# Three of four groups of each ungated MLP: the second product as seven half-size products, interleaved with the next group's first product

## The reference, cut to what matters

```python
def sqrelu_mlp(h, w_up, w_down):
    u = jnp.einsum('bsd,df->bsf', h, w_up)
    return jnp.einsum('bsf,fd->bsd', jnp.square(jax.nn.relu(u)), w_down)
...
x = x + sqrelu_mlp(rmsnorm(x, norm_mlp[l]), w_up[l], w_down[l])
```

## Time and profile before

| what | value |
|---|---|
| median of 3 runs | 1828.68 us (1828.45 to 1829.08) |
| the profiled execution | 1827.43 us |
| its span, first to last instruction | 1825.6 us |
| mean granted TensorE clock | 0.994 |
| PE busy | 1777.6 us, 97% |
| DVE busy | 959.8 us, 53% |
| ACT busy | 749.0 us, 41% |
| POOL busy | 104.7 us, 6% |

### The profile page before, as it was taken

One profiled execution on the slowest core, in us unless ns is written; L12 is line 12 of the kernel. 1 busy time (PEld: TensorE's weight loads), 2 busy tenths in 40 slices (PEclk: granted clock), 3 DMA queues, 4 the chain that ended last, 5 costly groups with the idle time before them and its releaser, 6 DMA issues.

```text
span 1825.6 us, 21577 instructions
## 1 busy us (share of the span) xinstructions
PE 1777.6 (97%) x8447; PEld 1460.1 (80%) x8447; DVE 959.8 (53%) x1740; ACT 749.0 (41%) x1475; POOL 104.7 (6%) x151
## 2 busy tenths in 40 slices
PE   8999999999999999989999999999999999999998
PEld 7887888888887777767888888878787788888886
DVE  6656443434344667765434434379986544244345
ACT  7433342323233666754233323243767533223223
POOL 0000010101010021011010101000000000000000
PEclk9999999999999999999999999999999999999999
DMA  7222223333323212112333332323100333333331
GB/s 246 78 80 81 81 95 102 103 94 94 97 98 86 70 49 68 47 47 81 94 97 99 93 104 93 104 71 103 51 19 1 95 106 98 93 96 101 96 101 58
DMA packets 195748, 158.30 MB, mean 87 GB/s; under 512 B 5248, under 2 KB 161280, under 8 KB 195648
## 3 DMA queue, kind: packets, MB, share of 16 engines
q1 hardware_dynamic: 194240, 154.16, 27.4%
q0 software_dynamic: 400, 1.25, 0.3%
q10 hardware_dynamic: 1008, 1.53, 0.2%
HBM read 154.81 MB, written 2.10 MB: 86 GB/s over the span
## 4 chain that ended last, share of the span: by engine, by line
PE 89%; DVE 6%; ACT 3%; issue 1%; DMA 0%; POOL 0%; DVEq 0%; SPq 0%; ACTq 0%
PE ps L736 29%; PE ps L738 28%; PE ps L737 28%; PE ps L1171 1%; PE ps L792 1%; ACT sb L1635 1%; PE ps L1065 0%; DVE sb L1855 0%; DVE sb L1853 0%; ACT sb L1375 0%; DVE sb L1881 0%; PE ps L851 0%; DVE sb L2265 0%; DVE sb L2218 0%; PE ps L1036 0%
## 5 line engine op out<-in xcount | busy, mean ns | idle before, releaser
L736 PE MATMUL ps<-sb,sb 128*128 128x512 f32 (+3 forms) x2547 | 976.0, 389 | 9.2 <-ACT sb L1635 5.2
L738 PE MATMUL ps<-sb,sb 128*128 128x512 f32 (+3 forms) x2547 | 956.8, 380 | 0.0
L737 PE MATMUL ps<-sb,sb 128*128 128x512 f32 (+3 forms) x2547 | 956.3, 380 | 0.0
L736 PEld LDWEIGHTS ps<-sb,sb 128*128 128x128 f32 (+1 forms) x2547 | 472.8, 188 | 116.0 <-issue 13.6
L738 PEld LDWEIGHTS ps<-sb,sb 128*128 128x128 f32 (+1 forms) x2547 | 472.3, 188 | 91.2
L737 PEld LDWEIGHTS ps<-sb,sb 128*128 128x128 f32 (+1 forms) x2547 | 472.9, 188 | 85.9 <-issue 0.2
L1855 DVE TENSOR_TENSOR sb<-sb,sb 128x512 fp32r<-128x512 f32 x532 | 348.7, 695 | 342.7 <-ACT sb L1375 341.6
L1375 ACT ACTIVATE sb<-sb 128x512 fp32r<-128x512 f32 x532 | 305.9, 622 | 432.1 <-PE ps L738 430.7
L2073 DVE TENSOR_TENSOR sb<-sb,sb 128x512 fp32r<-128x512 f32 x64 | 68.1, 1064 | 176.9 <-ACT sb L1524 176.6
L1534 ACT ACTIVATE sb<-ps 128x512 f32<-128x512 f32 x64 | 38.3, 598 | 208.6 <-PE ps L738 208.6
L664 POOL TENSOR_TENSOR sb<-sb 128x512 f32<-128x512 f32 x64 | 66.8, 1043 | 786.5 <-ACT sb L1534 786.5
(11 more groups left out here) (210 smaller groups left out, 982.5 us busy)
## 6 DMA issues: line engine op xcount, KB each, us to landing
sb<-in_w_up SPq DMA_DIRECT2D x86, 512.0 KB, 3.9
sb<-in_w_down SPq DMA_DIRECT2D x86, 512.0 KB, 3.9
sb<-in_w_gate SPq DMA_DIRECT2D x22, 512.0 KB, 3.7
sb<-in_a_w_in SPq DMA_DIRECT2D x20, 512.0 KB, 3.7
sb<-in_w_in SPq DMA_DIRECT2D x20, 512.0 KB, 3.6
sb<-in_w_o SPq DMA_DIRECT2D x16, 512.0 KB, 3.9
sb<-in_w_mem_kv SPq DMA_DIRECT2D x8, 512.0 KB, 7.5
sb<-in_w_out SPq DMA_DIRECT2D x8, 512.0 KB, 3.9
```

The costliest lines, as they stand in the source:

```text
L736: mm(ps, lh, rh, start=start, stop=False, **k)
L737: mm(ps, lh, rl, start=False, stop=False, **k)
L738: return mm(ps, ll, rh, start=False, stop=stop, **k)
```

## The change

Groups 0, 1 and 2 of each MLP compute the second product as seven products of half size in each dimension (256 tokens by 512 features by 512 columns) of sums of quarters, in a form of Strassen's scheme; group 3 keeps the old second product. Product j of group g (`P`) and tile j of group g+1's first product (`U`) take turns on PE, with two tiles behind product 6.

- A product is two slabs of 12 matmuls each. The weight quarters are loaded by SP as eight DMAs of 256 KB a group into buffers `DB` of their own. DVE forms eight half-quarter sums of weights (`T`, 128x1024) and four sums of quarters of the activation (`S`, 128x1024).
- DVE evicts each `U` tile with relu and the norm factor in one instruction (`r`), ACT squares into `HF` (`q`), and the high and low parts of the seven left operands are written by ACT and DVE over 1024 columns at a time (`h`). DVE reads each product's two banks (`rd`).
- POOL no longer works in the MLPs. PE transposes the norm factor into bank 7 and ACT copies it to `RB` in each MLP (`spread`), behind tile 1 of group 0. ACT squares the last two token tiles of `X` ahead of turns 4 to 7.
- `weights` is written to convert the slabs of a set `WIDE` in one instruction (`parts = 2`), and all others in two.

The diff, cut to what matters:

```diff
+    PRODUCTS = [(4, 2, "11", 0), (6, 5, "21", 0), (4, 0, "T2", 2), (6, 1, "11", 1), (2, 6, "12", 3), (6, 3, "22", 0),
+                (2, 4, "21", 4)]
...
+        for m in range(8):
+            up_tile(l, 0, m)
+        for g in range(3):
+            for j in range(7):
+                PS[l, g, j] = len(slabs)
+                for a in range(2):
+                    QSLAB[len(slabs)] = (l, g, j, a)
+                    slabs.append(([], 2, 512, None, 0))
+                for m in [j] if j < 6 else [6, 7]:
+                    up_tile(l, g + 1, m)
...
+    WIDE = {i for i in QSLAB} | {i for k, i in SL.items() if k[0] == "up" and k[2] > 2}
...
+        for g in range(3):
+            n = g + 1
+            last = g == 2
+            plan += [("P", g, 0), ("U", n, 0), up(n, 0), ("r", g, 7), ("q", g, 7), ws(g, 1, 0), ("S", g, 1), ("h", g, 1),
+                     ws(g, 1, 1), ("rd", g, 0), ("S", g, 2)]
+            plan += [("P", g, 1), ("U", n, 1), up(n, 1), ("r", n, 0), ("h", g, 2), ws(g, 2, 0), ("h", g, 3), ws(g, 2, 1),
+                     ("rd", g, 1), ("S", g, 4)]
+            plan += [("P", g, 2), ("U", n, 2), up(n, 2), ("q", n, 0), ("r", n, 1), ("q", n, 1), ("h", g, 4), ws(g, 3, 0),
+                     ("T", g, 3, 0), ws(g, 3, 1), ("rd", g, 2), ("T", g, 3, 1)]
+            plan += [("P", g, 3), ("U", n, 3), up(n, 3), ("r", n, 2), ("q", n, 2), ("h", g, 5), ws(g, 4, 0), ws(g, 4, 1),
+                     ("rd", g, 3), ("T", g, 4, 0), ("T", g, 4, 1)]
+            plan += [("P", g, 4), ("U", n, 4), up(n, 4), ("r", n, 3), ("q", n, 3), ("h", g, 6), ws(g, 5, 0), ws(g, 5, 1),
+                     ("rd", g, 4)]
+            if last:
+                plan += [("hc", 0), ("hc", 1), ("fold", 0, 1)]
...
+            plan += [("P", g, 6), ("U", n, 6), ("U", n, 7), up(n, 6), ("r", n, 5), ("q", n, 5), up(n, 7)]
...
+                plan += [ws(n, 0, 0), ("rd", g, 6), ("r", n, 6), ("q", n, 6), ("T", n, 1, 0), ws(n, 0, 1), ("T", n, 1, 1),
+                         ("T", n, 2, 0), ("T", n, 2, 1)]
...
+        def load_quarter(l, g, b):
...
+            for a in range(2):
+                if g > 0:
+                    q.wait_ge(S("w_lo"), 2 * (PS[l, g - 1, j] + a) + 2)
...
+                e.dma_start(DB[b][a][:, :].rearrange("p (k c) -> p k c", k=2), src).then_inc(S(f"db{b}_{a}"), 16)
...
-            for m in range(32):
-                z = m % 2
-                q.wait_ge(S("relu"), 32 * l + m + 1)
-                q.wait_ge(S("h_lo"), 32 * l + m - 1)
-                TTT(T2[:, z, :], T1[:, z, :], T1[:, z, :], ALU.mult).then_inc(S("relu2"), 1)
...
+            def product(g, j):
+                b, out, _, _ = PRODUCTS[j]
+                ah, al = AR[(7 * g + j) % 4]
+                q.wait_ge(S("h_lo"), h_done(l, g, j))
+                for a in range(2):
+                    _, wh, wl = next_slab()
+                    for t in range(2):
...
+                        for r in range(2):
+                            k, x, w = 2 * a + r, slice(128 * t, 128 * t + 128), slice(512 * r, 512 * r + 512)
+                            m = mm3(banks[b + t][:, :], ah[:, k, x], al[:, k, x], wh[:, w], wl[:, w],
+                                    k == 0 and j in (0, 1, 3, 4), k == 3, skip=True)
+                    m.then_inc(S("w_used"), 1)
...
-            for x in range(at["lo"], 2 * min(to, NSLAB) + half):
-                i, h = x // 2, x % 2
+            while at["lo"] < 2 * min(to, NSLAB) + half:
+                i, h = at["lo"] // 2, at["lo"] % 2
+                parts = 2 if i in WIDE else 1
...
+                elif kind == "r":
...
+                    stt(T1[:, m % 2, :], banks[u_bank(g, m)][:, :], 0.0, RB[:, :], ALU.max, ALU.mult).then_inc(S("relu"), 1)
```

More of the change, by code:

```diff
@@ L382, in build @@
+    PLAN_M = [mlp_plan(l) for l in range(2)]
     CV_GROUPS = [range(0, 10), range(10, 20), range(20, 31)]
@@ L921, in mlp, with free @@
             turn_first(X, job)
-            def free(m):
-                if m < 4:
+            def free(g, m):
+                if g == 0 and m < 4:
                     q.wait_ge(S("res"), base - 4 + m + 1)
-                elif m % 8 < 4:
-                    q.wait_ge(S("res"), base + 8 * (m // 8) - 4 + m % 8 + 1)
-                else:
[L930 to L944, removed]
@@ new lines, in mlp, with bank_free @@
+            for step in PLAN_M[l]:
+                if step[0] == "U":
+                    g, m = step[1:]
+                    tile_t(Ah, Al, job, u_bank(g, m), lambda: free(g, m),
+                           turn_in_tile(X, job) if (g, m) == (0, 0) else no_step)
+                elif step[0] == "spread":
+                    q.wait_ge(S("turn_lo"), 8 * JOB[job] + 8)
+                    spread(X, job)
+                elif step[0] == "P":
+                    product(*step[1:])
+            for n in range(2):
+                order = [2, 3, 4, 5, 6, 7, 0, 1]
+                def bank_free(t):
+                    if n == 1 and t < 2:
+                        q.wait_ge(S("relu"), 32 * l + 31 + t)
+                    else:
+                        q.wait_ge(*out_done(l, 2, 6 if n == 1 else 2 if t < 2 else 5, t % 2))
+                tile_n(CH["down", l, n], Bh, Bl, lambda k: q.wait_ge(S("h_lo"), h_done(l, 3, order.index(k))),
+                       (4, 0)[n], bank_free, behind=behind if n == 1 else no_step)
@@ L1513, in mlp @@
                 turn(job, Ah, job, k)
+            for t in range(2, 4):
+                square(X, job, t)
             weights(SL["up", l, 0] + 2)
@@ L1516, in mlp @@
                 turn(job, Ah, job, k)
[L1517 to L1540, removed]
+            rsqrt(job, 4)
@@ new lines, in mlp @@
+            for step in PLAN_M[l]:
+                if step[0] == "w":
+                    weights(step[1])
+                elif step[0] == "spread":
+                    spread(1 + l)
+                elif step[0] == "q":
+                    g, m = step[1:]
+                    q.wait_ge(S("relu"), 32 * l + 8 * g + m + 1)
+                    if g > 0:
+                        q.wait_ge(S("h_lo"), h_done(l, g - 1, 3 if m < 4 else 6))
+                        q.wait_ge(S("hs"), 4 * (3 * l + g - 1) + 4)
+                    act(HF[:, m, :], T1[:, m % 2, :], ACT.Square).then_inc(S("h_sq"), 1)
+                elif step[0] == "h":
+                    g, j = step[1:]
+                    q.wait_ge(*a_ready(l, g, j))
+                    q.wait_ge(*a_free(l, g, j))
+                    act(AR[(7 * g + j) % 4][0], A_OF[j][0], ACT.Copy).then_inc(S("h_hi"), 1)
+                elif step[0] == "hc":
+                    m = step[1]
+                    q.wait_ge(S("h_sq"), 8 * (4 * l + 3) + m + 1)
+                    q.wait_ge(S("w_used"), PS[l, 2, 3 + m // 2] + 2)
+                    act(Bh[:, (m + 2) % 8, :], HF[:, m, :], ACT.Copy).then_inc(S("h_hi"), 1)
@@ L1542, in scalar_program @@
+            for n in range(2):
+                for j in range(4):
+                    weights(CH["down", l, n].first + j + 3)
         mlp(0)
@@ L1807, in scalar_program @@
                 if m == 0:
-                    spread(2)
+                    spread(4)
                 if m > F0[g]:
@@ L2069, in mlp @@
                 turn(job, Ah, Al, job, k)
[L2071 to L2088, removed]
+            stats(job)
@@ new lines, in a_sum @@
+            def a_sum(g, k):
+                a11, a12, a21, a22 = (HF[:, 4 * p:4 * p + 4, 256 * t:256 * t + 256] for t in range(2) for p in range(2))
+                d, x, y, op = {1: (a21, a21, a22, ALU.add), 2: (a11, a21, a11, ALU.subtract),
+                               3: (S3B[:, :, :], a11, a21, ALU.subtract), 4: (a12, a12, a11, ALU.subtract)}[k]
+                q.wait_ge(S("h_sq"), 8 * (4 * l + g) + (4 if k == 3 else 8))
+                if k in (2, 4):
+                    q.wait_ge(S("hs"), 4 * (3 * l + g) + (2 if k == 2 else 3))
+                    q.wait_ge(S("h_lo"), h_done(l, g, 0 if k == 2 else 1))
+                tt(d, x, y, op).then_inc(S("hs"), 1)
@@ new lines, in mlp @@
+            for step in PLAN_M[l]:
+                kind = step[0]
+                if kind == "w":
+                    weights(step[1])
+                elif kind == "r":
+                    g, m = step[1:]
+                    n = 32 * l + 8 * g + m
+                    q.wait_ge(S("spread"), 2 + l)
+                    q.wait_ge(S("w_used"), SL["up", l, 8 * g + m] + 1)
+                    q.wait_ge(S("h_sq"), n - 1)
+                    stt(T1[:, m % 2, :], banks[u_bank(g, m)][:, :], 0.0, RB[:, :], ALU.max, ALU.mult).then_inc(S("relu"), 1)
+                elif kind == "T":
+                    weight_sum(*step[1:])
+                elif kind == "S":
+                    a_sum(*step[1:])
+                elif kind == "h":
+                    g, j = step[1:]
+                    q.wait_ge(S("h_hi"), h_done(l, g, j))
+                    hi, lo = AR[(7 * g + j) % 4]
+                    tt(lo, A_OF[j][0], hi.bitcast(F32), ALU.subtract).then_inc(S("h_lo"), 1)
```

(21 more changed lines are left out.)

225 lines of the change are left out of this document (174 added, 51 removed).

## The result

The changed kernel took 1796.75 us (median of 4 runs, 1794.85 to 1797.48); the kernel before, run beside it, 1828.87 (1828.45 to 1829.08). The ratio is 0.9823, 95% interval 0.9806 to 0.984. Predicted were 1797.2 us in a range of 1795 to 1808.

The account below looks back on a forecast made before the run. PE's matmul count was taken as the only limit in the MLPs. Terms -32.6 + 0.7 + 0.4 gave -31.5 us, with DVE and DMA at 0: 1828.7 - 31.5 = 1797.2 us, range 1795 to 1808.

Parts of the forecast that it names:

- Matmuls, -32.6: PE, groups 0 to 2 of both MLPs: 144 fewer matmuls at 0.2265 us each, -32.6 us.
- `spread`, +0.7: PE in each MLP: four added transposes delay the next matmul by 0.36 us, twice, +0.7 us.
- Squares ahead of the turns, +0.4: ACT's two squares before turn 4 delay PE's fifth `mm3` by 0.2 us in each MLP, +0.4 us.
- DVE, 0: Mixed steps: DVE's 61.3 us fit in a group's 81.6, PE waits 0; upper bound without overlap +6 us.
- The busy times forecast: Sign of being right, whole kernel: DVE busy about 1130 us, ACT 800, POOL 38.
- the break-even: DVE's chain in a group reaches the old 87.0 us if its operations are 1.24 times as dear; below, the change wins.
- Rival (b): DVE becomes the bound by its SBUF accesses; at `h_lo`'s factor 1.53, 105 us a group, some 1935 us; chance 0.04.
- DMA, 0: Weight loads in the MLPs: same bytes in smaller pieces land within a step, cost 0; one late load a group, 17 us.

## Why the prediction was right

**Matmuls, -32.6.** Right: 48 fewer of each of the three, +32.2 (2 either way) when they were put back.

**`spread`, +0.7.** A little short: it measures 0.9. The four transposes start at 234.62 and the next matmul at 234.98, 0.36 us as priced, but the step of three matmuls that follows takes 0.77 us (234.98 to 235.75) instead of 0.68. The trace of the kernel before has the same behind its turns (225.96 to 226.72 is 0.76), and I had left it out. That is 0.46 us each time.

**Squares ahead of the turns, +0.4.** Mis-sized, it measures 0.2: the sixth three-matmul step, which began 4.84 us after the first before (222.58 to 227.42), began 4.91 after it (222.18 to 227.09), and from the tenth on (7.57 and 7.68) the delay stays at 0.11 us; in the second MLP it is 0.08. The two squares held ACT for 2.3 us, not 2.5: they start at 222.47 and turn 4 at 224.78. The working took 1.24 us a square, the distance of two starts; the row that it names, 217.61 to 218.75, gives 1.14.

Measured for the two MLPs together: 31.5. With these two terms as measured the sum is -32.6 + 0.9 + 0.2 = -31.5, and my own is the same because their errors cancel, which is luck.

**DVE, 0.** Right in price (61.3 us in 81.6 by hand, 62.2 in 81 measured), in the order of the steps (11.2 us by hand, 11.31 from the same zero) and in the slack (over 3 us by hand, 3.2): one more wide operation a product is hidden, two are not. The busy times forecast, 1130, 800 and 38, were 1136, 808 and 38. That the break-even lies at operations 1.24 times as dear fits roughly: two more operations a product are 7 x 2.4 = 16.8 us on 61.3, 27% more, and cost 39 us, 7 more than the whole gain. Operations that were themselves dearer throughout were not tried.

**Rival (b).** My price for DVE beside POOL carried a factor of 1.53 over to all operations, 105 us a group; the real thing with four squares a tile was +11 us a group. The factor of `h_lo` was the average of an operation that was issued close behind a POOL square in every tile. With 256 squares (266 us at 1.04 each) DVE lost 141 us in all, and the operations that read PSUM lost nothing (679 ns).

**DMA, 0.** The value was right and its working was not. It took the quarter loads for 256 KB that land in 2.9 us, under 10 of 10.9 us in a step even one behind another; they are 512 KB and land in 4.8 us (median, at most 10.1), so that the fullest steps ask for three of 512 KB, 3 x 3.9 = 11.7 us by the same sum. What carried the term is that the loads are issued ahead: up slabs land in 4.1 us instead of 3.9, and no row shows PE or ACT waiting for a load in an MLP. A late load was not tried.

**Left open.** How much of the loss with two and three subtractions is the lower clock behind PE's pauses, and what a load that comes late would cost.

## What to carry to other kernels

Where PE is busy without a gap, trading matmuls for work on engines with idle time pays matmul for matmul, as long as the helper's list, including its pauses for other engines, fits. Its busy time alone does not tell. A step may run over by what the slack in front of the bound engine covers (here 11.69 us of 10.88, with 3.2 us of slack); seven dear steps in a row may not. Lay the dear steps beside steps that give the helper time: the same work in a bad order cost 43 us where the trade had won 32. Beyond the knee nearly every added microsecond shows; within it nothing does, and polishing there (wider conversions, earlier or later squares) is worth nothing that these runs can tell.

## What the runs showed of the hardware

A DVE operation with two SBUF inputs and a POOL operation on SBUF hold each other up: 0.855 against 0.690 us on average for DVE's 512 columns, 1.417 against 1.04 for POOL's, with four squares a tile; DVE reading PSUM and one SBUF tile stayed at 0.68. A wide operation (1024 columns) on DVE takes 1.22 us, and one that waits for nothing starts 1.13 us after it (377.89 to 379.02).

TensorE kept its full clock (1.00) through both MLPs while it had no pause; with two subtractions added, and PE idle for 11.3 of 258 us, it fell to 1.2 GHz for three stretches of 3.4 us.
